# A long convolution's first taps and two key products moved between engines in a fused transformer kernel

## What is computed

```
z = rmsnorm(h, g_mix) @ w_in
conv_val, conv_gate, rwkv_in, gate_logits = split(z)
y_a = conformer_conv(conv_val, conv_gate, ...)   # u = val * sigmoid(gate); 31-tap depthwise causal conv
y_b = rwkv7_mix(rwkv_in, ...)                    # r, k, v, decay; recurrence wkv7_scan over tokens
gate_a, gate_b = split(sigmoid(gate_logits))
h = h + (gate_a * y_a + gate_b * y_b) @ w_o
h = h + peer_ffn(rmsnorm(h, g_ffn), ...)
```

## Time and profile before

| | us |
|---|---|
| median of 3 runs (1616.02 to 1619.24) | 1616.18 |
| the profiled execution | 1617.77 |
| its span, first to last instruction | 1616.0 |
| TensorE busy in it | 1517.0 (94%) |
| VectorE, ScalarE, GpSimd busy | 1078.8, 827.4, 379.3 |

### The profile page before, as it was taken

How to read it: one execution, slowest core, us unless ns; L and a number is a source line. 1 busy time by engine, 2 the same in 40 slices (tenths; PEclk the granted TensorE clock), 3 DMA queues, 4 the chain that set the end, 5 groups by cost and what they waited for, 6 DMA issues and landing times.

```text
span 1616.0 us, 32177 instructions
## 1 busy us (share of the span) xinstructions
PE 1517.0 (94%) x11588; PEld 1389.2 (86%) x11588; DVE 1078.8 (67%) x1785; ACT 827.4 (51%) x1427; POOL 379.3 (23%) x168
## 2 busy tenths in 40 slices
PE   5998879999788998889999999999999999999998
PEld 4976669999678988788999999999999888888886
DVE  3426458777558788765578897899998444544444
ACT  3435445555455522255365656666766444445444
POOL 1210112222113201012223324312221222222221
PEclk8998999999889999999999999999999999999999
DMA  6630125556324500045545555544434556665664
GB/s 234 233 110 24 59 73 181 181 183 183 104 91 131 161 11 28 3 144 182 169 134 194 169 179 178 161 136 141 143 130 134 176 184 194 185 187 186 182 194 143
DMA packets 66231, 234.86 MB, mean 145 GB/s; under 512 B 8200, under 2 KB 9240, under 8 KB 66160
## 3 DMA queue, kind: packets, MB, share of 16 engines
q1 hardware_dynamic: 65760, 232.31, 45.0%
q0 software_dynamic: 400, 1.59, 0.3%
HBM read 232.80 MB, written 1.06 MB: 145 GB/s over the span
## 4 chain that ended last, share of the span: by engine, by line
PE 78%; issue 9%; DVE 7%; ACT 2%; POOL 2%; DMA 1%; SPq 0%; DVEq 0%; ACTq 0%; POOLq 0%
PE psum L686 40%; PE psum L1377 22%; PE psum L700 4%; PE psum L1343 4%; POOL w_lo L524 2%; DVE big L1650 2%; PE psum L669 1%; PE psum L744 1%; PE psum L986 1%; PE psum L1036 1%; PE psum L858 1%; ACT w_hi L510 1%; PE psum L1120 1%; DVE big L1749 1%; DVE w_lo L524 1%
## 5 line engine op out<-in xcount | busy, mean ns | idle before, releaser
L686 PE MATMUL psum<-x_hi,w_hi 128*128 128x256 f32 (+1 forms) x2152 | 627.5, 292 | 40.1 <-DVE x_lo L1432 12.9
L686 PE MATMUL psum<-x_lo,w_hi 128*128 128x256 f32 (+1 forms) x2152 | 616.2, 286 | 0.0
L524 POOL TENSOR_TENSOR w_lo<-ring,w_hi 128x1024 fp32r<-128x1024 f32 x141 | 348.9, 2475 | 1126.6 <-ACT w_hi L510 1126.6
L686 PE MATMUL psum<-x_hi,w_lo 128*128 128x256 f32 (+1 forms) x2152 | 612.6, 285 | 0.0
L510 ACT ACTIVATE w_hi<-ring 128x1024 fp32r<-128x1024 f32 x424 | 445.4, 1051 | 97.2 <-PE psum L686 82.5
L524 DVE TENSOR_TENSOR w_lo<-ring,w_hi 128x1024 fp32r<-128x1024 f32 x283 | 352.7, 1247 | 160.0 <-ACT w_hi L510 156.6
L686 PEld LDWEIGHTS psum<-x_hi,w_hi 128*128 128x128 f32 x2152 | 413.1, 192 | 50.0 <-issue 30.9
L686 PEld LDWEIGHTS psum<-x_hi,w_lo 128*128 128x128 f32 x2152 | 415.9, 193 | 0.0
L686 PEld LDWEIGHTS psum<-x_lo,w_hi 128*128 128x128 f32 x2152 | 414.1, 192 | 1.7 <-issue 1.4
L2079 DVE TENSOR_TENSOR h_lo<-big,h_hi 128x256 fp32r<-128x256 f32 x128 | 69.3, 542 | 163.0 <-ACT h_hi L2504 163.0
L1377 PE MATMUL psum<-w_hi,h_hi 128*128 128x512 f32 x512 | 160.9, 395 | 0.0
(11 more groups left out here) (316 smaller groups left out, 1752.0 us busy)
## 6 DMA issues: line engine op xcount, KB each, us to landing
ring<-experts SPq DMA_DIRECT2D x256, 512.0 KB, 3.6
ring<-w_ffn SPq DMA_DIRECT2D x66, 512.0 KB, 3.6
ring<-w_in SPq DMA_DIRECT2D x46, 512.0 KB, 3.7
ring<-w_mid SPq DMA_DIRECT2D x24, 512.0 KB, 3.5
ring<-w_out SPq DMA_DIRECT2D x16, 512.0 KB, 3.5
ring<-w_q SPq DMA_DIRECT2D x16, 512.0 KB, 4.1
big<-w_cmp SPq DMA_DIRECT2D x8, 512.0 KB, 5.8
big<-bias_rows POOLq DMA_DIRECT2D x1, 1536.0 KB, 8.7
```

Source lines behind the costliest of these rows:

```text
L524: eng.tensor_tensor(w_lo[:, n % RING, :], ring[:, n % RING, :], w_hi[:, n % RING, :].bitcast(F32), ALU.subtract).then_inc(low_ready2 if n ...
L686: mm = pe.matmul(dst, w[:, slot, k * P:(k + 1) * P], x[:, k, t0:t0 + width], start=(n == 0), stop=(n == 3 * len(chunks) - 1))
```

## The change

- The two key products go from GpSimd to VectorE, between its splits of tiles 17 and 19.
- The gate and value blocks of the convolution alternate as tiles 14 to 21 (4, 0, 5, 1, 6, 2, 7, 3), and the copy of a gate block applies the sigmoid. The one sigmoid over four blocks is gone.
- `glu` is made block by block (`glu_block`): blocks 0 and 1 after tile 20's split, blocks 2 and 3 before tile 24's. Gate 0's evacuation waits for the fourth.
- `conv_pair` takes the pair as an argument. Ten calls for pair 0 alone stand between the two halves of `glu`; ten calls leave the scan: three and one in group 0, four, one and one in group 1. After these ten, the calls alternate as before until pair 0 has its 31 taps.

```diff
-            for s in range(17, 24):
+            low(17)
+            dve.tensor_tensor(kappa_end, k_new, e_end, ALU.mult).then_inc(kappa_ready, 1)
+            low(18)
+            dve.tensor_tensor(kappa, k_new, e_neg, ALU.mult).then_inc(kappa_ready, 1)
+            for s in range(19, 21):
                 low(s)
+
+            def glu_block(m):
+                dve.wait_ge(in2_copied, 16 + 2 * m)
+                dve.tensor_tensor(glu[:, m, TAPS - 1:], zs[:, m], zs[:, 4 + m], ALU.mult).then_inc(glu_ready, 1)
+
             dve.wait_ge(pads_zeroed, 1)
-            dve.wait_ge(glu_sig, 1)
-            dve.tensor_tensor(glu[:, :, TAPS - 1:], zs[:, 0:4], zs[:, 4:8], ALU.mult).then_inc(glu_ready, 1)
-            dve.wait_ge(glu_ready, 1)
+            for m in (0, 1):
+                glu_block(m)
+            for s in range(21, 24):
+                conv_pair(0)
+                conv_pair(0)
+                low(s)
+            for _ in range(4):
+                conv_pair(0)
+            for m in (2, 3):
+                glu_block(m)
...
-            def conv_pair():
+            def conv_pair(pair=None):
...
-                t, pair = n // 2, n % 2
+                if pair is None:
+                    pair = n % 2 if taps_of[n % 2] < TAPS else 1 - n % 2
+                t = taps_of[pair]
                 if t > 0:
-                    dve.wait_ge(conv_tap, n - 1)
+                    dve.wait_ge(conv_tap, last_of[pair])
+                else:
+                    dve.wait_ge(glu_ready, 2 * pair + 2)
+                taps_of[pair], last_of[pair] = t + 1, n + 1
...
-                for _ in range((7, 6)[tg]):
+                for _ in range((4, 2)[tg]):
                     conv_pair()
...
-                for _ in range((3, 4)[tg]):
+                for _ in range((2, 3)[tg]):
                     conv_pair()
...
                     if c == 0:
-                        conv_pair()
                         stack_zero()
...
-                    act.activation(z2[:, row, 1:T2 + 1], psum[:, s % 4, 0:T2], ACT.Copy).then_inc(in2_copied, 1)
+                    act.activation(z2[:, row, 1:T2 + 1], psum[:, s % 4, 0:T2],
+                                   ACT.Sigmoid if row >= 4 else ACT.Copy).then_inc(in2_copied, 1)
...
-            act.wait_ge(in2_copied, 22)
-            act.activation(z2[:, 4:8, 1:T2 + 1], z2[:, 4:8, 1:T2 + 1], ACT.Sigmoid).then_inc(glu_sig, 1)
...
                 if g == 0:
-                    act.wait_ge(glu_ready, 1)
+                    act.wait_ge(glu_ready, 4)
```

More of the change, by code:

```diff
@@ L409, in bass_transformer_pair @@
         gn_spread = sem("gn_spread")
-        glu_sig = sem("glu_sig")
         bonus_scaled = sem("bonus_scaled")
@@ L480, in bass_transformer_pair @@
         keys_loaded = sem("keys_loaded")
-        IN2_ROWS = [20, 21] + list(range(12, 16)) + list(range(8, 12)) + list(range(16, 20)) + list(range(8))
+        IN2_ROWS = [20, 21] + list(range(12, 16)) + list(range(8, 12)) + list(range(16, 20)) + [4, 0, 5, 1, 6, 2, 7, 3]
         N_SHIFT = 14
@@ L625, in _ @@
             pool_splits(B_IN2 + 2, B_IN2 + 17)
[L626 to L629, removed]
             pool_splits(B_IN2 + 17, B_MID + 10)
@@ L1636, in _ @@
             taps_done = [0]
-            def conv_pair():
+            taps_of, last_of = [0, 0], [0, 0]
+            def conv_pair(pair=None):
                 n = taps_done[0]
@@ L2592 @@
     w2 = tiles(g["w_in_2"])
-    w2_in = w2[[20, 21] + list(range(12, 16)) + list(range(8, 12)) + list(range(16, 20)) + list(range(8))]
+    w2_in = w2[[20, 21] + list(range(12, 16)) + list(range(8, 12)) + list(range(16, 20)) + [4, 0, 5, 1, 6, 2, 7, 3]]
     branches = tiles(np.concatenate([g["w_conv_out_2"], g["w_rwkv_out_2"]], 0))
```

## The result

The changed kernel took 1605.57 us (median of four runs, 1603.75 to 1608.19) against 1616.1 before (1615.7 to 1619.24): a ratio of 0.9925, interval 0.9906 to 0.9945. That is 10.5 us faster. The sign was as forecast (1609.7, a gain of 6.5), the size was not: the gain is 4 us larger. A second measurement of both gave the same: 1606.5 against 1616.51, 0.9931 (0.9907 to 0.9954).

The account below looks back on a forecast made before the run. TensorE was taken to bound the kernel (78% of the chain), so only removed TensorE waits pay. Scan -6.6 and gate stage +0.1 gave -6.5 from 1616.18: 1609.7 us, 8-in-10 range 1604.8 to 1613.2.

Parts of the forecast that it names:

- The wait at tile 14 and the clock there: Tile 14: TensorE restarts 2.3 us earlier, its wait falling from 3.74 to 1.45, and the clock holds.
- The clock term: After tile 14's wait: 1.6 us lost to the low clock before, regained because the clock holds.
- VectorE's queue from the split of 16 to that of 25: Gate stage: 29.7 us of VectorE work from 512.15, so tile 25's split starts near 542.0, 2.6 late for TensorE.
- the rival's condition: Gate-stage rival, chance 0.22: free chains and one collision missed, 3.4 us together, let the stage keep 4.9; 1604.7 us.
- GpSimd takes its 2.4 us before the split of 26: Gate stage: GpSimd's split of tile 27 goes ahead of VectorE's split of 26, which then ends at 548.35.
- Gate 4 starts at 548.4, where it did before: Gate stage: the late split of tile 26 leaves gate 4's start unchanged, before being 548.34.
- of 5.0 us earned, 5.0 are given back: Gate stage gains nothing; bounds from 5.0 us gained to 3.3 lost.
- ScalarE's wait for the fourth glu block: Before gate 0: ScalarE waits for that block, with the splits of tiles 25 to 27 behind it.
- The scan: Ten calls fewer: both TensorE waits (1.84, 3.12) and 1.63 of low clock go, 6.6 us in all.
- the second rival: Scan rival, chance 0.16: second wait stays in part and the clock falls, gain 3.4 us; 1612.8 us.
- The slower rival: Gate stage, chance 0.07: each of ten calls costs 0.8 more, tile 25's split comes 6.6 us later; 1617.8 and beyond.
- That nothing would be freed at 506: Tile 14 rival: TensorE still restarts at 510; time within 1 us of forecast, 1610.5, chance counted with the forecast.

Follow-up runs that it names:

- the pause kernel: Changed kernel with one wait added: VectorE's second key product waits for the end of the first; 1608.59 us, ratio 0.9946.
- the kernel with the calls back: Changed kernel with the ten convolution calls back in the scan, the other edits kept; 1610.46 us, ratio 0.9971.
- The kernel with the forced order: Changed kernel with one wait added: VectorE's split of tile 26 waits for the end of the taps right before it; 1609.01 us in one run.
- seven calls: Changed kernel with seven calls, not ten, ahead of tile 25, last two glu blocks earlier, each gate waiting for its own block; 1604.39 us, ratio 0.9921.

## Why the prediction was right in its direction and short in its size

*The wait at tile 14 and the clock there: right.* -2.29 against -2.3. The clock term was taken as 1.6. From tile 14 to the start of tile 17, after is 1.5 shorter than the profile that I read. From tile 14 to gate 0 it is 0.95 shorter, since tile 18 has a new wait. Against the two other profiles of before it is 2.2 shorter, since their clock stays low for longer (tile 15 starts 5.61 after tile 14 in one of them, 4.57 in the profile that I read). That the clock would hold after 1.45 was less certain than I made it. The same profile of before has a fall after 1.69, at the start of the second group's `grams`, which I left out (the second line has the columns of the earlier trace rows):

```profile
615.58 7.52 PE L1027 MATMUL psum<-big 64*128 64x128 f32 x80 [1.69 <-DVE sq L1807]
```

```profile
615.00:620.00 5.00, 4.42 (x39) 4.42 (x41) 2.66 (x6) 0.80 (x3) 0.00 (x0) 0.66 0.00 0
```

*VectorE's queue from the split of 16 to that of 25: nearly right.* 29.7 worked out, 29.06 measured, with VectorE busy for nearly all of it (columns as in the earlier trace rows):

```profile
509.40:538.46 29.06, 28.79 (x232) 28.40 (x231) 28.21 (x38) 11.31 (x18) 9.84 (x3) 1.00 0.51 165
```

All three collisions came, 1.9 to 2.4 each. A chained call costs 0.12: eight taps with three such calls took 5.89, eight with none 5.54. The second of these lines, from after, answers to the earlier trace rows:

```profile
527.49 1.86 DVE L1651 SCALAR_TENSOR_TENSOR big<-big 128x272 f32<-128x272 f32 x4
529.27 1.22 DVE L523 TENSOR_TENSOR w_lo<-ring,w_hi 128x1024 fp32r<-128x1024 f32 x1
530.40 5.89 DVE L1651 SCALAR_TENSOR_TENSOR big<-big 128x272 f32<-128x272 f32 x8
```

The Trainium skill (VectorE: DVE Perf Modes, The DRAIN you can't avoid) says that a semaphore costs nothing extra, which it measured on eight `tensor_copy`. For these taps that does not hold. So the rival's condition, free chains and a collision missed, did not come about, though its result did in part. TensorE waited 1.34 at tile 25, not 2.6: the split came 0.8 earlier than worked out, and TensorE was 0.75 later (0.54 of it at tile 18, whose wait the forecast did not have, by the pause kernel, which has no such wait).

*"GpSimd takes its 2.4 us before the split of 26": this step failed.* In after VectorE ran four taps and then the split of 26 past the waiting GpSimd instruction. From it followed "Gate 4 starts at 548.4, where it did before" and "of 5.0 us earned, 5.0 are given back". Given back were 2.4 (the kernel with the calls back). Measured from tile 14, gate 4 came at 37.6 instead of 40.5 (548.4 - 507.86), and the scan at 50.5 instead of 52.8 (560.65 - 507.86). The kernel with the forced order has gate 4 at 39.7 and the scan at 51.8. So of the 2.3 us that after is ahead of the forecast at the scan's start, the order explains 1.3. Another 0.5 is that tile 25 started earlier than worked out (34.7 after tile 14, not 543.1 - 507.86 = 35.2); the last 0.5 is spread over the tiles behind and not explained. Against the mean of the three profiles of before, after is 3.05 ahead: the further 0.8 is no step of mine, but the profile that I read, which was the shortest of the three in this stage.

*ScalarE's wait for the fourth glu block: there, but its price was left out.* It idled 5.77 ahead of gate 0 and made three gates in one go. Its rounding of tile 25 stands behind gate 0 and ended at 538.43; the two calls that VectorE has behind that block ended at 538.50, and the split of tile 25 started at 538.46. So two paths of the same length led from the fourth block to that split, and my sum had only VectorE's. In all six executions with the ten calls ahead, the split starts 0.03 to 0.04 after that rounding, so fewer taps behind the block alone would hardly have made it earlier; no run tested that by itself.

*The scan: right.* 6.6 worked out (10.51 - 12 x 0.41 is 5.6 and not 5.5, which changes nothing). Three profiles each give 5.5; all profiles with the calls in the scan (six, mean 118.2) against all with them out (eight, mean 111.7) give 6.5. Both waits went whole, group 1's `add_power` came when it was worked out to, and the second rival (half the gain) is ruled out. Some of group 0's gain went again in the first profile to a gap of 1.50 between two products, which the trace calls issue; it was 0.2 to 1.3 in the other executions.

*The sum.* 2.3 + 0.75 + 5.5 to 6.5 is 8.6 to 9.6 of the 10.0 to 10.5 that the medians show. The remainder is as large as what two levels of the clock behind the scan make between executions (up to 1.5 and 1.5), which no step of mine could have given; with the ten calls in or out these levels came unequally often, and this part stays open. The slower rival was far off: no chained call cost 0.8. That nothing would be freed at 506 is ruled out by the wait of 1.43.

The first part of the gap between 6.5 and 10.5, about 3 us, is placed: it is the gate stage, 1.3 of it by the order, 0.8 by the execution that I read. The second, 0.4 to 1.9, is not.

## What to carry to other kernels

An engine's idle time is room for moved work only up to the next thing that is waited for behind it. Count the queue from one split to the next, move as many calls as fit, and stop: seven calls here left the gate stage 2.4 us shorter than ten, with the same time in the scan. Ask of each engine that waits for the moved work what it has to do before the next tile: here ScalarE's path was as long as VectorE's.

Where two engines exclude each other, which goes first at one boundary decides 1 to 2 us. If the forecast hangs on it, price both orders and keep both in the range; I had one of them, as a fact.

One profile of the kernel before is one execution. The stage that I read as 25.62 was 26.8 to 26.9 in the two later ones, and the levels behind the scan moved 1.5 us each with no change of code.

## What the runs showed of the hardware

GpSimd's turn at the shared port is not first come, first served. A waiting GpSimd split was passed by a VectorE product that was issued after it (4.76 at 512.84), and by a split behind taps (3.80 at 540.95). The Trainium skill (SBUF — State Buffer, Who interferes with whom) has it that whoever issues first gets the port pair for the whole instruction and the other blocks; the blocking agrees, the order does not say enough, since the blocked one can lose again. A pause of VectorE let GpSimd in each of the two times it was tried (3.57 and 2.63). But in before it got in without one, between `alpha` and the split of tile 14, and between a split and the taps behind it; in after too:

```profile
550.07 4.04 POOL L523 TENSOR_TENSOR w_lo<-ring,w_hi 128x1024 fp32r<-128x1024 f32 x1 [5.33 <-ACT w_hi L509]
```

That split was passed by one more tap and by the split of VectorE behind it, and entered ahead of the next tap. The exact rule stays open.

The clock after a wait of 2.2 us fell in some executions and held in others of the same program (0.66 and 1.00 in the same 4 us). After waits of 1.3 to 1.5 us at tiles 14 and 25 it held in each profile of the changed kernel, after one of 1.87 (the forced order) too; after 1.99 at tile 25 (the pause, and the key products back on GpSimd) it fell, and after 3.7 at tile 14 it fell in each kernel that had such a wait. But the length of the wait alone does not decide: after the 1.84 in the scan's first group it held in four profiles (1.00 from 580 to 585 in before) and fell in two (0.66 from 575 to 580 with only the key products moved), and after the 1.69 ahead of the second group's `grams` it fell in twelve of fourteen.
